# Latent norms summed per token and turned back in the first mixer, and an inverse moved ahead of a weight remainder in the second

## The reference, cut to what matters

```python
proj = h @ w_in                      # 1024 -> q, k, v, q_lat (256), kv_lat (128), k_rope
q  = rmsnorm(q_lat,  q_norm)  @ w_q_up
kv = rmsnorm(kv_lat, kv_norm) @ w_kv_up
def rmsnorm(x, gain):                # per token, over the features
    return x * rsqrt(mean(x * x) + 1e-6) * gain
```

## Time and profile before

| | |
|---|---|
| median of 3 runs | 2318.56 us |
| profiled execution | 2320.85 us, of which the span of instructions is 2319.1 us |
| TensorE busy in matmuls | 2264.2 us, 98% of the span, mean granted clock 0.99 |
| VectorE, ScalarE, GpSimd busy | 1330.4, 791.9 and 1105.1 us |
| first mixer, projections | about 60 to 158 us of the span |
| first mixer, attention and output | 158 to 352 us |
| mixture of experts | 352 to 1740 us |
| second mixer; feed-forward | 1740 to 1952 us; 1952 us to the end |

### The profile page before, as it was taken

How to read it: one execution, slowest core, us unless ns; L and a number is a source line. 1 busy time by engine, 2 the same in 40 slices (tenths; PEclk the granted TensorE clock), 3 DMA queues, 4 the chain that set the end, 5 groups by cost and what they waited for, 6 DMA issues and landing times. The chain is left out here.

```text
span 2319.1 us, 30967 instructions
## 1 busy us (share of the span) xinstructions
PE 2264.2 (98%) x10633; PEld 1856.6 (80%) x10633; DVE 1330.4 (57%) x2459; ACT 791.9 (34%) x1225; POOL 1105.1 (48%) x727
## 2 busy tenths in 40 slices
PE   9889999999999999999999999999999999999999
PEld 7667787888888888888888888878887678888887
DVE  6476667899764222222248888888875755333322
ACT  4254532232333222222233333333343444222211
POOL 0059653455788888888027888778601300000000
PEclk8999999999999999999999999999999999999999
DMA  6123236634577777666758999999932102222232
GB/s 263 64 91 110 82 119 239 232 132 146 132 182 191 145 145 145 144 146 144 273 191 320 358 374 345 348 351 362 342 142 100 35 10 82 100 98 91 95 100 86
DMA packets 177647, 409.00 MB, mean 176 GB/s; under 512 B 55712, under 2 KB 97568, under 8 KB 170528
## 3 DMA queue, kind: packets, MB, share of 16 engines
q1 hardware_dynamic: 115296, 315.53, 40.4%
q0 software_dynamic: 61696, 84.12, 14.0%
q10 hardware_dynamic: 576, 8.39, 1.0%
HBM read 347.00 MB, written 60.95 MB: 176 GB/s over the span
## 5 line engine op out<-in xcount | busy, mean ns | idle before, releaser
L1737 DVE TENSOR_TENSOR w_lo<-w_raw,w_hi 128x1024 fp32r<-128x1024 f32 x228 | 280.0, 1228 | 479.3 <-ACT w_hi L1619 369.9
L59 PE MATMUL ps<-p_h_hi,w_hi 128*128 128x512 f32 x1152 | 453.4, 394 | 1.5 <-POOL w_lo L1444 0.8
L1472 POOL DMA_INDIRECT gates<-p_tok,p_g_cell x256 | 414.4, 1619 | 78.0 <-issue 78.0
L60 PE MATMUL ps<-p_h_lo,w_hi 128*128 128x512 f32 x1152 | 448.7, 389 | 0.0
L61 PE MATMUL ps<-p_h_hi,w_lo 128*128 128x512 f32 x1152 | 448.6, 389 | 0.0
L1619 ACT ACTIVATE w_hi<-w_raw 128x1024 fp32r<-128x1024 f32 x143 | 151.6, 1060 | 470.6 <-PE ps L61 461.1
L59 PE MATMUL ps<-w_hi,p_w_hi 128*128 128x512 f32 x768 | 301.1, 392 | 6.6 <-DVE p_w_lo L1886 5.3
L60 PE MATMUL ps<-w_lo,p_w_hi 128*128 128x512 f32 x768 | 301.3, 392 | 0.0
L61 PE MATMUL ps<-w_hi,p_w_lo 128*128 128x512 f32 x768 | 300.2, 391 | 0.0
L59 PEld LDWEIGHTS ps<-p_h_hi,w_hi 128*128 128x128 f32 x1152 | 216.5, 188 | 47.4 <-POOL w_lo L1444 2.5
L61 PEld LDWEIGHTS ps<-p_h_hi,w_lo 128*128 128x128 f32 x1152 | 216.3, 188 | 45.3
(11 more groups left out here) (413 smaller groups left out, 3783.4 us busy)
## 6 DMA issues: line engine op xcount, KB each, us to landing
w_raw<-U_d SPq DMA_DIRECT2D x128, 512.0 KB
w_raw<-V_d SPq DMA_DIRECT2D x128, 512.0 KB
activations<-p_q SPq DMA_DIRECT2D x128, 192.0 KB
w_raw<-w_gu_d SPq DMA_DIRECT2D x44, 512.0 KB, 3.5
w_raw<-w_ada_d SPq DMA_DIRECT2D x32, 512.0 KB, 3.5
gates<-p_dense POOLq DMA_DIRECT2D x16, 1024.0 KB, 7.1
p_big<-activations SPq DMA_DIRECT2D x8, 1536.0 KB
p_h_lo<-activations SPq DMA_DIRECT2D x8, 1536.0 KB
```

The lines of the kernel that those rows point to most:

```text
L59: pe.matmul(out, w_hi, x_hi, start=start, stop=False)
L60: pe.matmul(out, w_hi, x_lo, start=False, stop=False)
L1472: pool.indirect_dma_start(g_cells, bass.IndirectOffsetOnAxis(ap=g_cell[:, t, s:s + 1], axis=0), tok[:, 2, t, s:s + 1], None, compute_op=AL ...
L1737: dve.tensor_tensor(lo[:, r % 2, :], raw[:, r, :], hi[:, r % 2, :].bitcast(F32), ALU.subtract).then_inc(lo_ready, 1)
```

## The change

In the first mixer a new class `LatentNorms` replaces two uses of `Norms` and of `Normed.dve`. The sums are now one number per token on the partitions (the squares are the stationary operand, a column of ones the moving one), four matmuls of one column for each latent. The inverse is made on 128x4 numbers, the root widens each to 128 columns, and four transposes turn it back into a PSUM bank of 128x512. Scaling is one instruction with gain and inverse together (`dve_scaled`). The steps stand earlier: squares of the third latent, first sums, inverse and root at j = 3, second sums and inverse and root and the first spread at j = 4, second spread at j = 5; the query latents are scaled at j = 4 and the key/value latent at j = 5, where they stood at 5 and 6. In the second mixer the final norm's inverse stays at unit 22, the weight remainder moves behind it to 23, the spread moves from 24 to 25, and the scaling from 25 to 26.

```diff
+class LatentNorms:
+    def square(self, act, n, src):
+        if n == 2:
+            act.wait_ge(self.summed, 1)
+        act.activation(self.sq[:, n % 2, :], src, ACT.Square).then_inc(self.squared, 1)
+    def sums(self, pe, n, ones_column):
+        squares = [0, 1] if n == 0 else [2]
+        pe.wait_ge(self.squared, squares[-1] + 1)
+        if n:
+            pe.wait_ge(self.step, 1)
+        for t in range(TT):
+            for i in squares:
+                mm = pe.matmul(self.columns[:, n * TT + t:n * TT + t + 1], self.sq[:, i % 2, t * P:t * P + P], ones_column,
+                               start=i == squares[0], stop=i == squares[-1])
+        mm.then_inc(self.summed, 1)
+    def inverse(self, dve, n):
+        r = self.r[:, n, :]
+        dve.wait_ge(self.summed, n + 1)
+        dve.tensor_scalar(r, self.columns[:, n * TT:n * TT + TT], 1.0 / ((2 - n) * P), EPS, ALU.mult, ALU.add).then_inc(self.step, 1)
+        dve.wait_ge(self.step, 2 * n + 1)
+        dve.reciprocal(r, r).then_inc(self.step, 1)
+    def root(self, act, n):
+        act.wait_ge(self.step, 2 * n + 2)
+        act.activation(self.wide[:, n, :].rearrange("p (t c) -> p t c", c=P),
+                       self.r[:, n, :].unsqueeze(2).broadcast_to([P, TT, P]), ACT.Sqrt).then_inc(self.rooted, 1)
+    def spread(self, pe, n):
+        pe.wait_ge(self.rooted, n + 1)
+        for t in range(TT):
+            c = slice(t * P, t * P + P)
+            mm = pe.transpose(self.banks[n][:, c], self.wide[:, n, c], self.ident)
+        mm.then_inc(self.spread_done, 1)
...
                     if j == KROPE:
-                        norms.sums(pe, ones[:], 1, KD, 2)
+                        latent_norms.sums(pe, 0, ones[:, 0:1])
+                    if j == K:
+                        latent_norms.sums(pe, 1, ones[:, 0:1])
+                    if j in (K, Q0):
+                        latent_norms.spread(pe, j - K)
                     if KROPE < j:
                         n = j - 1 - KROPE
                         rotation.pe(pe, n, tab["pair_mla" if n == 0 else "pair_swa"][:], kept, j)
-                    if j == K:
-                        norms.sums(pe, ones[:], 2, KD + 2, 1)
...
                     if j == KVLAT:
                         act.wait_ge(kept, KVLAT + 1)
-                        norms.squares(act, KD, [lat[:, i, :] for i in range(3)])
+                        for i in range(2):
+                            latent_norms.square(act, i, lat[:, i, :])
+                    if j == KROPE:
+                        latent_norms.square(act, 2, lat[:, 2, :])
+                        latent_norms.root(act, 0)
                     if j == K:
-                        norms.root(act, 1)
+                        latent_norms.root(act, 1)
+                        normed.act(act, KD, latn_hi, 2)
                     if j == Q0:
-                        norms.root(act, 2)
-                        normed.act(act, KD, latn_hi, 2)
-                    if j == Q0 + 1:
                         normed.act(act, KD + 2, latn_hi[:, 2:3, :], 1)
...
+                    if j == KROPE:
+                        latent_norms.inverse(dve, 0)
                     if j == K:
-                        norms.inverse(dve, 1, KD + 2, 2 * P)
+                        latent_norms.inverse(dve, 1)
+                        dve.wait_ge(latent_norms.spread_done, 1)
+                        normed.dve_scaled(dve, lambda k: lat[:, k, :], ps[:, 7, :], lambda k: col("mla_q_norm", k), None,
+                                          latn_hi, latn_lo, KD, 2)
                     if j == Q0:
-                        norms.inverse(dve, 2, KD + 3, P)
-                        dve.wait_ge(norms.rstd_ready, 2)
-                        normed.dve(dve, KD, lambda k: lat[:, k, :], norms.rstd[:, 1, :], lambda k: col("mla_q_norm", k), None,
-                                   latn_hi, latn_lo, 2)
-                    if j == Q0 + 1:
-                        dve.wait_ge(norms.rstd_ready, 3)
-                        normed.dve(dve, KD + 2, lambda k: lat[:, 2, :], norms.rstd[:, 0, :], lambda k: col("mla_kv_norm"), None,
-                                   latn_hi[:, 2:3, :], latn_lo[:, 2:3, :], 1)
+                        dve.wait_ge(latent_norms.spread_done, 2)
+                        normed.dve_scaled(dve, lambda k: lat[:, 2, :], ps[:, 4, :], lambda k: col("mla_kv_norm"), None,
+                                          latn_hi[:, 2:3, :], latn_lo[:, 2:3, :], KD + 2, 1)
...
-        SPLIT_AT, SUMS_AT, INVERSE_AT, ROOT_AT, SPREAD_AT, SCALE_AT = 13, 21, 22, 23, 24, 25
+        SPLIT_LO_AT = 23
+        SPLIT_AT, SUMS_AT, INVERSE_AT, ROOT_AT, SPREAD_AT, SCALE_AT = 13, 21, 22, 23, 25, 26
...
                     if i == INVERSE_AT:
+                        final.inverse(dve)
+                    if i == SPLIT_LO_AT:
                         stream.split_lo(dve, 12)
-                        final.inverse(dve)
```

More of the change, by code:

```diff
@@ L394, in spread, with __init__ @@
         mm.then_inc(self.spread_done, 1)
+class LatentNorms:
+    def __init__(self, ctx, nc, tag, columns, banks, sq, wide, ident):
+        self.columns, self.banks, self.sq, self.wide, self.ident = columns, banks, sq, wide, ident
+        self.r = ctx.enter_context(nc.sbuf_tensor(tag + "_r", [P, 2, TT], F32))
+        sem = lambda n: nc.alloc_semaphore(tag + "_" + n)
+        self.squared, self.summed, self.step, self.rooted, self.spread_done = (sem("squared"), sem("summed"), sem("step"), sem("rooted"),
+                                                                              sem("spread"))
+    def square(self, act, n, src):
[28 more added lines that the diff above has]
+        mm.then_inc(self.spread_done, 1)
 class Normed:
@@ L404, in __init__ @@
         self.lo_done = nc.alloc_semaphore(tag + "_lo_done")
[L406 to L429, removed]
     def act(self, act, first, hi, blocks, shift=None):
@@ L438, in act, with dve_scaled @@
             ins.then_inc(self.hi_done, 1)
-    def dve_scaled(self, dve, x, rstd, gain, shift, hi, lo):
+    def dve_scaled(self, dve, x, rstd, gain, shift, hi, lo, first=0, blocks=KD):
         def rest(k):
-            dve.wait_ge(self.hi_done, k + 1)
-            full = self.full[:, k % 2, :]
+            n = first + k
+            dve.wait_ge(self.hi_done, n + 1)
+            full = self.full[:, n % 2, :]
             if shift is None:
@@ L450, in rest @@
             ins.then_inc(self.lo_done, 1)
[L452 to L455, removed]
+        for k in range(blocks):
+            n = first + k
+            if n >= 2:
+                dve.wait_ge(self.lo_done, n - 1)
+            dve.scalar_tensor_tensor(out=self.full[:, n % 2, :], in0=x(k), scalar=gain(k), in1=rstd, op0=ALU.mult,
                                      op1=ALU.mult).then_inc(self.full_ready, 1)
@@ L458, in dve_scaled @@
                 rest(k - 1)
-        rest(KD - 1)
+        rest(blocks - 1)
 class Rotation:
@@ L741, in mixer1 @@
         rotation = Rotation(ctx, nc, "a_rot", [ps[:, 2, :], ps[:, 3, :]])
+        latent_norms = LatentNorms(ctx, nc, "a_lat", ps[:, 5, 0:2 * TT], [ps[:, 7, :], ps[:, 4, :]], norms.sq, norms.rstd, ident[:])
         turn = Turn(ctx, nc, "a_turn", [ps[:, 2, :], ps[:, 3, :]], ident[:])
```

## The result

The changed kernel took 2301.53 us (median of four runs, 2298.9 to 2305.28) against 2319.44 us for the kernel before it on the same chip: a ratio of 0.992, 95% interval 0.9898 to 0.9942. The prediction was 2303.1 us. The profiled execution took 2298.9 us, with a span of 2297.1 us; its counterpart of before took 2320.85 us and 2319.1 us. The two profiles thus stand 22.0 us apart, the medians 17.9 us.

A forecast was written before the change was run, and what follows sets the result against it. TensorE was taken to lose time in the first mixer's projections to norm waits and the lower clock after them. Gains of 10.9 + 2.5 + 2.1 = 15.5 us from 2318.56 gave 2303.1 us; range 2298.5 to 2310.5.

The forecast's parts named there:

- The removed waits, less the new work: First mixer's projections: 13.0 us of lost time regained, less 2.1 us of added TensorE work, 10.9 us; bounds 9 and 11.5.
- the five periods: First mixer: five dense blocks with pairings at 6.33 us each, 31.65 us undisturbed against 44.69 measured, so 13.0 us lost.
- The query products: Latent query products, first mixer: GpSimd starts earlier and collides less with VectorE, 2.5 us gained; bounds 0 and 4.6.
- Rival (a): Latent query products: the collision with GpSimd stays as dear, 13.0 us gained, 2305.6 us; chance 0.14.
- The second mixer: Final norm there: the wait for the root goes, the last scaling comes later, net 2.1 us gained; bounds 0.8 and 2.8.
- its two terms: Second mixer: 2.6 us gained from the removed root wait, 0.5 us lost on the last scaling before the output projection.
- (b): First mixer: the wait moves to the second spread, 1.8 us in hand, 8.3 us given back, 2311.4 us; chance 0.07.
- (c): First mixer's attention: GpSimd's weight blocks set its pace and the gain is given back there, 2316 us; chance 0.05.
- (d): First mixer, steps 3 to 5: small matmuls and transposes bring the lower clock, 2334.7 us, slower; chance 0.04.
- the counted margin of 1.8 us: First mixer, step 4: root ready at most 5.8 us after the block, second spread wanted at 7.6, so its latency is hidden.

The follow-up runs named there:

- the one with the third block later: Changed kernel with GpSimd's third modulation block held until ScalarE copied out the first latent key block, and final norm scaling from unit 25: 2300.41 us, ratio 0.9907.
- the first run above: Changed kernel with the second mixer's steps put back as before, only the latent norms changed: 2304.41 us against 2321.2, ratio 0.9928.

## Why the prediction was right, and where it was off

**The removed waits, less the new work: 10.9 us predicted, 10.53 measured.** It is 41.37 us in each of the seven profiles whose code up to there is that of the kernel after. The term that was too small is that of the five periods: the distance of two pairings is 6.45 us in the kernel after (92.25, 98.70, 105.14 and 111.60), not the 6.33 of the earlier trace rows, 0.6 us in five, where the prediction allowed 0.05 to 0.1 behind the new work. It is not a price of pairing behind that work, for the same matmuls are slower ahead of it too, where TensorE's queue is the same in both kernels. These rows (first the kernel after, then before) start the 45 matmuls that end at the first sums, at 70.23 and 71.88:

```profile
59.73 0.40 PE L59 MATMUL ps<-a_in_hi,w_hi 128*128 128x512 f32 x1
```

```profile
61.65 0.40 PE L59 MATMUL ps<-a_in_hi,w_hi 128*128 128x512 f32 x1
```

They take 10.50 and 10.23 us, 0.233 and 0.227 us each. All nine profiles with the new form have 10.50, the four with the old form 10.23 or 10.24, and behind the experts the two kinds agree again (0.227 us around 2000 us). So it comes with the program and not with the steps; what makes it stays open. The sums and the second spread take 7.74 us with their block (85.35 - 77.61), where 7.6 were counted. The prediction said that the order of each queue counts and costed it so; the runs with order or form alone show how much: order 8.4 us, form 2.45.

**The query products: 2.5 us predicted, 3.29 measured.** The mechanism was the predicted one: GpSimd started at 105.46, where 107 was counted and 105.4 is what that becomes with the start 1.65 us earlier; the waits left sum to 1.97 us (below 2). The overlap with GpSimd fell to 11.8 us, a little below the 13 that were counted. The prediction counted one wait of 2.88 us and not the 0.82 us before it, so its starting point was low by that. The waits fell from 3.70 to 1.97 us, and the clock stayed at 1.00 in spite of what is left, which the prediction had kept between its bounds and which gave the other 1.6 us. The term scatters: 30.70 to 30.98 us in five profiles with the same code there, 31.92 in that of the remainder moved alone, where the waits were 0.27, 1.41 and 1.13 us. Rival (a), that the collision stays as dear, is out by the 3.29 us themselves; the run that holds GpSimd back shows that another 2.4 us were to be had.

**The second mixer: 2.1 us predicted, 1.86 measured**, its two terms as counted: 2.63 us gone, 0.61 of it by the remainder's move, and 0.58 us of new wait. What it had left out is the clock: in two of three profiles with the old wait it fell behind it, and this part was then worth 3.5 to 3.8 us. The whole kernel can show this half only faintly (ratio 0.9985, up to 0.9998). Here the table load comes into play. The copy ahead of the load ends 0.02 us before it (1853.68 + 0.58, then 1854.28), the root starts 0.02 us behind it (1854.28 + 1.28, then 1855.58), and the root was ready 0.06 us before its spread. The Trainium skill (ScalarE: Activation LUTs, What ACT_TABLE_LOAD costs) has about 1380 ns of drain with the load. This trace does not agree for these rows: neither side of the load has room for it, and with it the spread would have had a wait.

**The rivals.** (b), a wait at the second spread: 1.86 us in hand, and the run that made the root 3.2 us later paid 1.43, so it would have had to be far later to matter. (c), a longer attention: 189.3 us, not longer. It can be provoked: GpSimd held back to the end of the query products makes it 196.5. (d), the clock: the sums and transposes ran at 1.00 and so did all behind them; refuted here.

**What was not predicted: about 6 us of the profiled pair, and some 2 to 3 us of the medians.** The parts sum to 15.7 us, and the medians stand 17.9 and 18.9 us apart. So the sum is as good as its parts, and that the time itself came within 1.6 us of 2303.1 is in part luck: the median of before moved up by 0.9 us with the fourth run, and parts that were not costed gave the rest. In the first attention, where I had counted no change, the clock fell near the end in the kernel before and not after (190.95 against 189.32 us):

```profile
288.00:298.00 10.00, 10.00 (x54) 9.56 (x53) 5.06 (x10) 5.16 (x9) 3.90 (x3) 0.66 0.03 13
```

```profile
271.00:281.00 10.00, 8.71 (x66) 7.81 (x64) 5.25 (x10) 5.30 (x9) 3.89 (x3) 1.00 0.14 55
```

In the thirteen profiles it fell in the four with the old form of the norms and the one with the third block later, and in none of the eight others. Thus it goes with the form of the norms (all four of the old form, one of nine of the new) and not with their order, and is worth 1.4 to 2.0 us. What decides stays open: neither the size of the wait nor the collision does. A third place is the second mixer's wait of 2.63 us, whose fall is told with the first run above; in the profiled pair it did not come. It may be part of what the medians have over the costed sum, but only profiles tell whether it came, so no run shows its share. Behind the experts there is another such place (1738 us in the kernel before, 1720 after), where the profiled pair also differs, by 1.7 us. There the fall goes with nothing: it is in the repeated change and not in its first profile, and it came in eight of the thirteen profiles, of kernels of either kind. The experts (1385 to 1397 us over all profiles) and the start scatter likewise: the first sums stand between 70.19 and 72.79 in those same seven. So the profiled pair flatters the change by chance in these stretches.

## What to carry to other kernels

Ask of a wait first what stands ahead of its releaser in that engine's queue: the narrow form of the norms gave 2.45 us by itself, the old form issued a step earlier 8.4. Count every wait in the stretch, not the longest alone. Such a change can be costed by adding up each engine's queue between two anchors and comparing when a result is ready with when it is wanted: the counted margin of 1.8 us measured 1.86, and an injected delay cost the delay less the margin. Reckon the freed engine's neighbours too (GpSimd's blocks came 16 us earlier here), and take single profiles apart by stretch before crediting an edit, since clock falls of 1.4 to 2 us come and go elsewhere. Take the length of a period from the kernel as it will be where you can: here it grew by 0.12 us for no reason in the steps.

## What the runs showed of the hardware

The granted clock did not follow the size of a wait: with a wait of 1.15 or 1.16 us at the same instruction it fell to 0.66 in two kernels and stayed at 1.00 in others, behind the same wait of 2.63 us in the second mixer it fell in two profiles of three, and the wait of 1.25 us that was injected at the second spread left it at full. VectorE and GpSimd held each other up: VectorE's product at 121.02 started inside a GpSimd product, took 1.77 us and ended 0.55 us after it, and GpSimd's 128x1024 product at 135.10, inside which two VectorE products ran in their usual 0.68 us, took 2.93 us where the one at 105.46, with VectorE idle nearly to its end, took 1.90. Ahead of the first sums the same 45 dense matmuls took 10.23 or 10.24 us in the four profiles with the old form of the norms and 10.50 in the nine with the new, though TensorE's queue up to there is the same in both. A table load of 1.28 us had 0.02 us of idle time on either side.
